# Last quarter of the MLP's down projection with tokens on the partitions, in a two-layer decoder step

## The reference

```python
D_MODEL, D_FF, ALPHA, LN_EPS = 1024, 4096, 4.0 ** 0.25, 1e-5

def _layer_norm(x, g, b):
    mu = jnp.mean(x, -1, keepdims=True)
    var = jnp.mean(jnp.square(x - mu), -1, keepdims=True)
    return (x - mu) * lax.rsqrt(var + LN_EPS) * g + b

    ff = jnp.square(jax.nn.relu(x @ P['w_up'])) @ P['w_down']
    x = _layer_norm(ALPHA * x + ff, P['ln3_g'], P['ln3_b'])
...
    z = x @ P['w_in']
```

## Time and profile before

| | us |
|---|---|
| median of 3 runs (lowest, highest) | 2308.52 (2303.39, 2311.03) |
| profiled execution | 2308.79 |
| its span | 2307.0 |
| tensor engine (PE) busy | 2240.0 |
| VectorE (DVE) busy | 1097.4 |
| ScalarE (ACT) busy | 432.2 |
| down projection, last quarter (L2367) | 512 product rows, 118.3 us |

### The profile page before, as it was taken

How to read it: one execution, slowest core, us unless ns; L and a number is a source line. 1 busy time by engine, 2 the same in 40 slices (tenths; PEclk the granted TensorE clock), 3 DMA queues, 4 the chain that set the end, 5 groups by cost and what they waited for, 6 DMA issues and landing times. The chain is left out here.

```text
span 2307.0 us, 32150 instructions
## 1 busy us (share of the span) xinstructions
PE 2240.0 (97%) x13494; PEld 1640.6 (71%) x13494; DVE 1097.4 (48%) x1951; ACT 432.2 (19%) x915; POOL 117.1 (5%) x208
## 2 busy tenths in 40 slices
PE   7999998999999999999999999989999999999997
PEld 5877765546865888888888777555478468888885
DVE  5652244655434544675166422535454264438643
ACT  2332122121211222100023311311113021220000
POOL 0111101100000000000002111000001000000000
PEclk9999998999999999999999999989999999999998
DMA  7111113243443122222242111132245322223221
GB/s 280 58 66 39 58 38 79 92 137 146 183 144 130 37 87 96 73 73 73 73 130 73 38 39 58 51 106 98 91 183 198 131 92 73 73 74 109 73 73 39
DMA packets 136335, 217.27 MB, mean 94 GB/s; under 512 B 33672, under 2 KB 67776, under 8 KB 136064
## 3 DMA queue, kind: packets, MB, share of 16 engines
q1 hardware_dynamic: 133888, 211.02, 26.5%
q10 hardware_dynamic: 2304, 4.20, 0.5%
HBM read 198.39 MB, written 14.58 MB: 92 GB/s over the span
## 5 line engine op out<-in xcount | busy, mean ns | idle before, releaser
L725 PE MATMUL psum<-xT,ring 128*128 128x256 f32 (+1 forms) x768 | 226.8, 422 | 0.1
L2266 PE MATMUL psum<-tmp 128*128 128x272 f32 x768 | 181.4, 393 | 0.0
L2266 PEld LDWEIGHTS psum<-tmp 128*128 128x128 f32 x768 | 145.8, 190 | 30.8 <-issue 0.8
L725 PEld LDWEIGHTS psum<-xT,ring 128*128 128x128 f32 x768 | 134.3, 193 | 36.4 <-issue 10.2
L677 PE MATMUL psum<-xT,ring 128*128 128x256 f32 (+1 forms) x512 | 120.3, 394 | 4.4 <-ACT big L1813 2.0
L722 PE MATMUL psum<-ring,ext 128*128 128x512 f32 x256 | 121.0, 608 | 2.9 <-ACT ext L1793 2.9
L2367 PE MATMUL psum<-big,ring 128*128 128x256 f32 (+1 forms) x512 | 118.3, 393 | 0.0
L677 PEld LDWEIGHTS psum<-xT,ring 128*128 128x128 f32 x512 | 96.3, 190 | 25.7 <-issue 4.6
L2685 PE MATMUL psum<-ring,big 128*128 128x512 f32 x256 | 113.1, 595 | 0.0
L825 PE MATMUL psum<-ring,big 128*128 128x512 f32 x256 | 111.9, 594 | 0.0
L2367 PEld LDWEIGHTS psum<-big,ring 128*128 128x128 f32 x512 | 97.0, 190 | 19.7
(11 more groups left out here) (494 smaller groups left out, 3586.7 us busy)
## 6 DMA issues: line engine op xcount, KB each, us to landing
ring<-in_w_down SPq DMA_DIRECT2D x16, 2048.0 KB, 7.6
ring<-in_w_in SPq DMA_DIRECT2D x14, 2048.0 KB, 8.6
ring<-in_w_up SPq DMA_DIRECT2D x14, 2048.0 KB, 7.5
big<-in_cache_mem_k SPq DMA_DIRECT2D x16, 1024.0 KB, 6.7
ring<-in_xa_wk SPq DMA_DIRECT2D x4, 2048.0 KB, 8.6
ring<-in_xa_wv SPq DMA_DIRECT2D x4, 2048.0 KB, 10.9
ring<-in_w_out SPq DMA_DIRECT2D x4, 2048.0 KB, 9.9
ring<-in_xa_wq SPq DMA_DIRECT2D x4, 2048.0 KB, 7.8
```

Source lines behind the costliest of these rows:

```text
L725: ins = pe.matmul(bank[:, :c.stop - c.start], wring[:, n % 2, k, i * P:(i + 1) * P], xTv[:, k, c], start=(k == 0), stop=(k == KC - 1))
L2266: ins = pe.matmul(ps[:, :HT], left[:, k, :], right[:, k, :], start=(k == 0), stop=(k == KH - 1))
```

## The change

The last quarter is computed with the tokens on the partitions: for each prompt tile a 128x128 block of `hT` is the weight and 256 columns of `w_down` move (`token_tile(T, r)`, 16 products for tile T and slab r). The result lands in PSUM as `down_residual` needs it, so the copy to `yT` and `turn_down(3, ...)` go. The sample tile is `token_sample(r)` in four column groups in bank 4; ScalarE copies the parts to `down_part`, and one product with `fold` adds them. Each tile has its own bank and `last_residual`. The norm's order of tiles becomes 0, 4, 1, 2, 3 (`place`), the turns in the next layer 4, 2, 3 (`LAST_TILES`). Layer 0's start keeps its order.

```diff
+        def place(ln, T):
+            return (0, 2, 3, 4, 1)[T] if ln and ln % 3 == 0 else T
+
+        def last_residual(v, key, T):
+            n = TILES[T][1]
+            x = xk[:n, T, 3 * W256:4 * W256]
+            ps = bk.take(v, key)
+            ins = v.scalar_tensor_tensor(x, x, ALPHA, ps[:n, 0:W256], ALU.mult, ALU.add)
+            bk.give(ins, key)
+            bk.given(v, key)
+            v.wait_ge(sig["v"], sig.up(v.bn_stats(stats4[:n, T, 3, :], x), "v"))
...
-                    bk.take(sp, ("down", 3, 1, 1))
+                    bk.take(sp, ("dt", 3, 3))
...
+            LAST_TILES = (2, 3, 4) if l == 0 else (4, 2, 3)
...
                     if i:
-                        turn_x_tensor(pe, bk, sig, LN0, i + 1, i + 1, (2, 3))
-                for g in range(2):
-                    bk.given(pe, ("xT", LN0, 4, g))
+                        T = LAST_TILES[i - 1]
+                        turn_x_tensor(pe, bk, sig, LN0, T, place(LN0, T), (2, 3))
+                for T in range(2, 5):
+                    for g in range(2):
+                        bk.given(pe, ("xT", LN0, T, g))
...
-                for half in range(2):
-                    for i, r in (((0, 0), (0, 1), (1, 0), (1, 1)), ((0, 1), (1, 1), (0, 0), (1, 0)))[half]:
...
-                        for k in range(2 * KC):
-                            ins = pe.matmul(ps, w[r][:, k, i * P:(i + 1) * P], hT[:, 2 * KC * r + k, c],
-                                            start=(r == half and k == 0), stop=(r != half and k == 2 * KC - 1))
...
+                def token_tile(T, r):
...
+                    for k in range(2 * KC):
+                        ins = pe.matmul(ps, hT[:, 2 * KC * r + k, t0:t0 + P], w[r][:, k, :], start=(first and k == 0),
+                                        stop=(not first and k == 2 * KC - 1))
...
+                def token_sample(r):
...
+                    for k in range(2 * KC):
+                        g = (k % 4) * NS
+                        ins = pe.matmul(ps[g:g + NS, :], hT[:, 2 * KC * r + k, SEQ:NT], w[r][:, k, :], start=(r == 0 and k < 4),
+                                        stop=(r == 1 and k >= 2 * KC - 4), skip_group_check=True)
...
+                token_tile(0, 0)
+                token_sample(0)
+                for pair in range(3):
+                    turn_down(SQ - 1, pair)
+                token_tile(0, 1)
+                token_sample(1)
+                token_tile(1, 1)
+                bk.given(pe, ("down", "part"))
+                ps = bk.begin(pe, ("dt", q, 4), 4)
+                bk.filled(pe.matmul(ps[:NS, 0:W256], const("fold"), down_part, start=True, stop=True), ("dt", q, 4))
+                token_tile(1, 0)
+                token_tile(2, 1)
                 if l < DEPTH - 1:
-                    for T in range(2):
-                        turn_x_tensor(pe, bk, sig, LN3, T, T, (2, 3))
-                for pair in (1, 2):
-                    turn_down(3, pair)
+                    turn_x_tensor(pe, bk, sig, LN3, 0, place(LN3, 0), (2, 3))
+                sig.up(token_tile(3, 1), "downread")
+                token_tile(2, 0)
+                if l < DEPTH - 1:
+                    turn_x_tensor(pe, bk, sig, LN3, 1, place(LN3, 1), (2, 3))
+                token_tile(3, 0)
...
-                for T in range(2):
-                    down_residual(v, ("dt", SQ, T // 2), SQ, T)
-                    ln_vector(v, sig, LN3, T, T)
+                for T in (0, 4, 1):
+                    last_residual(v, ("dt", SQ, T), T)
+                    ln_vector(v, sig, LN3, T, place(LN3, T))
...
-                down_half(3, 1, 1)
+                ps = bk.take(s, ("down", "part"))
+                bk.give(s.activation(down_part, ps[:, 0:W256], ACT.Copy), ("down", "part"))
```

More of the change, by code:

```diff
@@ L771, in head_scalar @@
                         turn_x_scalar(s, bk, sig, LN0, T)
-                ln_scalar(s, sig, LN0, 2, 2)
+                ln_scalar(s, sig, LN0, 2, place(LN0, 2))
                 for i in range(4):
@@ L775, in head_scalar @@
                     if i:
-                        turn_x_scalar(s, bk, sig, LN0, i + 1)
-                    if i < 2:
-                        ln_scalar(s, sig, LN0, i + 3, i + 3)
+                        turn_x_scalar(s, bk, sig, LN0, LAST_TILES[i - 1])
+                    if i == 0 or (i == 1 and l == 0):
+                        ln_scalar(s, sig, LN0, i + 3, place(LN0, i + 3))
                 for i in range(4):
@@ L783, in head_vector @@
             def head_vector(v):
-                for T in range(0 if l == 0 else 2, 5):
+                for T in range(5) if l == 0 else (2, 3):
                     if l == 0:
@@ L788, in head_vector @@
                     else:
-                        down_residual(v, ("last", "dt", 3, T // 2), 3, T)
-                    ln_vector(v, sig, LN0, T, T)
+                        last_residual(v, ("last", "dt", 3, T), T)
+                    ln_vector(v, sig, LN0, T, place(LN0, T))
             def first_loads(sp):
@@ L2069, in _ @@
                     for T, n in ((0, 2), (2, 2)):
-                        sp.wait_ge(sig["ln_done"], 5 * LN0 + T + n)
+                        sp.wait_ge(sig["ln_done"], 5 * LN0 + place(LN0, T + 1) + 1)
                         sp.dma_start(yp[:, T:T + n], xk[:, T:T + n, :]).then_inc(sig.dma("y"), 16)
@@ L2230, in build @@
             SQ = 3
-            DOWN_BANK = {(0, 0): 5, (1, 0): 6, (0, 1): 7, (1, 1): 0}
+            LAST_BANK = (5, 6, 7, 0)
+            down_part = cols(tmp, 2048 + 4 * KH * HT, W256)
             dsum = [xsum, cols(xT, 0, 4, KH, HT)]
@@ L2242, in turn_down @@
                 def turn_down(q, pair):
[L2244 to L2252, removed]
+                    bk.given(pe, ("dn", q, 0))
+                    bk.given(pe, ("dn", q, 6))
+                    bank = (7 * (18 + q)) % 8 if q < SQ - 1 else (1, 2, 3)[pair]
                     ps = bk.begin(pe, ("dt", q, pair), bank).rearrange("p (a c) -> p a c", a=2)
@@ L2378, in mlp_tensor @@
-                if l < DEPTH - 1:
-                    for T in range(2):
-                        turn_x_tensor(pe, bk, sig, LN3, T, T, (2, 3))
-                for pair in (1, 2):
-                    turn_down(3, pair)
+                def token_tile(T, r):
+                    if w[r] is None:
+                        slab_wait(pe, 25 + 2 * q + r)
+                        w[r] = cols(ring, ((25 + 2 * q + r) % 2) * KC * W512, 2 * KC, W256)
+                    key, t0 = ("dt", q, T), TILES[T][0]
+                    first = key not in bk.turn
+                    if first:
+                        bk.begin(pe, key, LAST_BANK[T])
+                    ps = psum[:, bk.turn[key][0], 0:W256]
+                    for k in range(2 * KC):
+                        ins = pe.matmul(ps, hT[:, 2 * KC * r + k, t0:t0 + P], w[r][:, k, :], start=(first and k == 0),
+                                        stop=(not first and k == 2 * KC - 1))
+                    if not first:
+                        bk.filled(ins, key)
+                    return ins
@@ new lines, in token_sample @@
+                def token_sample(r):
+                    key = ("down", "part")
+                    if key not in bk.turn:
+                        bk.begin(pe, key, 4)
+                    ps = psum[:, bk.turn[key][0], 0:W256]
+                    for k in range(2 * KC):
+                        g = (k % 4) * NS
+                        ins = pe.matmul(ps[g:g + NS, :], hT[:, 2 * KC * r + k, SEQ:NT], w[r][:, k, :], start=(r == 0 and k < 4),
+                                        stop=(r == 1 and k >= 2 * KC - 4), skip_group_check=True)
+                    if r:
+                        bk.filled(ins, key)
@@ L2495, in mlp_scalar @@
                 square(FC - 1, (3, 6))
[L2496 to L2503, removed]
                 for q in range(SQ):
@@ L2510, in mlp_scalar @@
                     bk.give(s.activation(yT[:, 1, T_HALVES[0]], ps[:, :HT], ACT.Copy), ("dn", q, 0))
[L2511 to L2515, removed]
-                down_half(3, 1, 1)
+                ps = bk.take(s, ("down", "part"))
+                bk.give(s.activation(down_part, ps[:, 0:W256], ACT.Copy), ("down", "part"))
+                for T in (0, 4, 1):
+                    ln_scalar(s, sig, LN3, T, place(LN3, T))
                 if l < DEPTH - 1:
@@ L2983, in _ @@
             def _(v):
-                for T in range(2, 5):
-                    down_residual(v, ("last", "dt", 3, T // 2), 3, T)
-                    ln_vector(v, sig, LN0, T, T)
+                for T in (2, 3):
+                    last_residual(v, ("last", "dt", 3, T), T)
+                    ln_vector(v, sig, LN0, T, place(LN0, T))
             @block.scalar
             def _(s):
-                for T in range(2, 5):
-                    ln_scalar(s, sig, LN0, T, T)
+                for T in (2, 3):
+                    ln_scalar(s, sig, LN0, T, place(LN0, T))
             @block.sync
             def _(sp):
```

(6 more changed lines are left out.)

## The result

| | before | after |
|---|---|---|
| median (lowest to highest of 20 runs), us | 2307.57 (2303.37 to 2311.26) | 2311.85 (2308.74 to 2314.69) |
| ratio of the runs | | 1.0019, 95% interval 1.0012 to 1.0026 |
| span of the profiled execution, us | 2307.0 | 2307.4 |

The change costs 4.3 us (0.19%), where I had forecast 3 us less, and 2311.85 lies above the range, which ended at 2310.5. It is slower, though by less than the 0.3% that the prediction took as its bound.

A forecast was written before the change was run, and what follows sets the result against it. The tensor engine, busy 97% of the span, was taken as the bound except at the layer border and the tail. Layer 0 0.65 us slower and layer 1 3.7 us faster gave -3.05 us: 2305.5 us, range 2301 to 2310.5.

The forecast's parts named there:

- the 0.3% that the prediction took as its bound: Whole time: a measurement can tell about 0.3%, 6.9 us, from no change; the forecast gain of 3 us lay inside.
- the same 0.88 us: Border between layers: time from the start of the last transposes to the next layer's first product, taken as unchanged.
- any new wait of the tensor engine on "ln_done" or a bank: Profile after: a sign listed as showing the prediction wrong, beside a pass over 4 us or VectorE starting tile 2 early.
- Products, 0.9 us more a layer: Last quarter of the down projection, each layer: 61.1 us against 60.22, the sample tile eating up the prompt's saving.
- The skill's 2.38 for three column tiles: Sample passes: a page's speedup, 0.79 of ideal, would make the passes 4.35 us a layer instead of 3.4.
- The grouped products take turns (rival, 3%): Sample passes: four groups don't overlap, each row costs 0.2155 instead of 0.054 us, 20.7 us slower, 2326 us; chance 3%.
- SyncE's issue holds the border, 0.4 us: Border between layers: the block's border waits for SyncE's second weight slab issue, priced 0.4 us, between 0 and 0.8.
- Last turn of a full tile, 0.55 us: Next layer's turns, order 4, 2, 3: a full tile last instead of the short one costs 0.55 us more net.
- Layer 0 in all, 0.65 us more: Layer 0: border of -0.25 us plus the products' 0.9 us; bounds from 0.65 faster to 1.05 slower.
- Tail, 3.7 us less: Second layer's end: only tiles 2 and 3 behind the border, 4.6 us less; with the products' 0.9, 3.7 us faster.
- Tile 3 ready at its turn: Next layer's turns: tile 3's norm ends some 8 us after 1158, its turn comes at about 1174, so no wait.
- The clock: Tensor engine: its granted clock was read as high in nearly every slice.

The follow-up runs named there:

- the wait alone: The kernel before, with TensorE made to wait at layer 1's start for the bank of tiles 2 and 3; 2314.36 us against 2308.88, ratio 1.0031.
- the filled wait: The changed kernel with nine unused products put into free bank 4 at layer 1's start, the wait for bank 0 kept; 2309.85 us, ratio to before 1.0005.

## Why the prediction was wrong

The step that failed is the sentence on the border that "the same 0.88 us" pass from the last instruction to the next layer's first product. I asked whether the turned tiles were ready, whether SyncE was, and whether tile 3 would be normed by its turn. I did not ask which bank the next layer's first product writes. It is bank 0. Before, bank 0 held the last block of the old layout, and ScalarE's copy freed it at once. Now it is freed by VectorE's residual of tile 3, which stands behind the border and behind the whole norm of tile 2. With the 0.4 us for SyncE, the prediction had 1.3 us from the last product to the next; it was 5.3. The wait of 3.9 us and the half clock of 1.8 us behind it are what the kernels with the other bank, with the wait alone and with the filled wait showed. Together they are 5.7 of the 6.0 us that layer 0 came out over its forecast (6.65 against 0.65). In the list of what would prove it wrong stood 'any new wait of the tensor engine on "ln_done" or a bank'; the program would have given the place beforehand, and the prediction's own terms most of the wait: 0.52 us to VectorE's start, 3.73 for tile 2 and 0.41 for the residual, less the 1.3, are 3.4 us.

The other terms, point by point:

- *Products, 0.9 us more a layer:* 61.0 us in layer 1 against 61.1 forecast. A pass with both changes of form took 2.0 us: 1.86, and 0.1 us of a start later than the 6.90 us of the rows ahead of it. Right.
- *The skill's 2.38 for three column tiles:* by the estimate from the page "TensorE: Matmul & The Clock Gate" of the Trainium skill, section "Measured speedup vs the span model", a pass would take 2.2 us without its changes of form. The trace has 1.86 with the way out included, 3.8 times as fast as the 7.03 us of one group. The measurement decides: more than the estimate's 3.2 times.
- *The grouped products take turns (rival, 3%):* they don't. The kernel with one group shows that price, 7.03 us a pass.
- *SyncE's issue holds the border, 0.4 us:* 0.5 us, from 1.38 to 0.86. Right, a little small.
- *Last turn of a full tile, 0.55 us:* 0.65 us. Right.
- *Layer 0 in all, 0.65 us more, taken without the bank's wait:* with the other bank 1094.65 to 1176.56 us is 81.91 us against 80.87, 1.0 us more.
- *Tail, 3.7 us less:* 3.6 us, and for the named reason; that VectorE's work, not tile 2's sum, waits for the border was shown by moving it (2.9 us less at the end in the profile, 3.9 by the ratios).
- *Tile 3 ready at its turn:* right, but by other times. Its norm was put at some 8 us after 1158; it ended at 1170.65. ScalarE's part of it stood behind the copy of the first product of layer 1, which came late (1168.46), and VectorE was idle for 4.38 us ahead of its last row (L297, from 1169.36). Tile 3's turn came at 1180.30, so nothing waited.
- *The clock:* the prediction read it as high nearly everywhere and gave it no term. A gap of 5.15 us was not foreseen, nor was its second cost.

With the bank moved the kernel measures 2.0 us under before by the medians (0 to 4.4 by the interval), and its profile has 2.5 us less in the two places (1.04 - 3.56), of 3.05 forecast. The reasons held for what they covered, and one dependency outside them turned the sign.

## What to carry to other kernels

When results change the engine that drains them, list for each PSUM bank who writes it next, across the block's border too, and what stands ahead of the draining instruction in its engine's program. A tile that is complete early gains nothing while its consumer stands behind a barrier; move the consumer, not only the producer. Price a gap of several microseconds on the tensor engine at more than its length where rows show half clock behind such gaps, as it stood behind both long gaps here.

## What the hardware showed that was not expected

After the change the granted clock stayed at 1.00 while TensorE stood idle (1158 to 1163 us) and was at 0.50 from its first row on, for about 3 us. With the added wait it fell while TensorE was still idle, at about 1164.4 us, 0.7 us ahead of the first row, and stayed at 0.50 for about 7 us. The cost was 1.8 and 3.0 us on the same 32 rows. Gaps of 0.7 and 1.2 us at the same place left it at 1.00, and so did spare products in the gap. Idle time is not needed for a fall: the slow rows at 1455.55 us in the profile before ran at 0.50 with no idle row of TensorE ahead of them, and no run here tells why. The Trainium skill, page "TensorE: Matmul & The Clock Gate", section "What's actually happening", says that the clock is released by activity and knows two levels, 1.2 and 2.4 GHz. The 0.50 here is the lower one, so the trace agrees on the levels.
